# A two-layer encoder in 3-product fp32: five instead of four seven-product couples in each wide pair, other weight sums, and evictions by ScalarE

## The chip, the cores and the metric

One core of a Trainium2 chip runs the whole program. The metric is the device time of one execution in microseconds. The engines are TensorE (PE; its weight loads are PEld), VectorE (DVE), ScalarE (ACT), GpSimd (POOL) and SyncE (SP), whose queue issues the loads.

## The reference

Two layers over 256 positions of width 2048, all in float32. A layer is a mixing half (projection, windowed attention, pooling, output projection) and a feed-forward half. Only the feed-forward half changes here:

```
x = x + rms_norm(mixed, g_mix_post)
f = square(relu(rms_norm(x, g_ffn_pre) @ w_up)) @ w_down      # 2048 -> 8192 -> 2048
x = x + rms_norm(f, g_ffn_post)
```

## The kernel before

**Three matmuls for a product.** Each float32 operand is split into a high part, rounded to the fast format fp32r, and a low remainder. For weights ScalarE casts (`w_hi<-raw`), VectorE subtracts (`w_lo<-raw,w_hi`). A product of a 128x128 stationary block and a 128x512 moving block is three matmuls, high x high, high x low, low x high (`three`, L870). In what follows a "product" is these three.

**Groups.** D_FF = 8192 is done in four groups g = 0 to 3 of 2048 columns. In each, four up units compute `relu(h @ w_up)^2` (`turned_unit`; the last one, u = 3, is `last_unit` on the other engines), and then two *wide pairs* q = 0 and 1 multiply it by w_down: each pair makes 1024 output columns (two banks of 512 for each of two token tiles, `acc_pair[t][:, c]`) over the 16 k-tiles of the group. In group 3 the place of pair 1 is taken by two narrow units. So there are 7 wide pairs in a layer, 14 in all.

**Slots and couples.** A wide pair takes its 16 k-tiles as slots i = 0 to 15, one 128x1024 piece of w_down each. Plain slots take four products (t, c). Two neighbouring slots can be a *couple* (`seven`, L880): a 2x2x2 block product with seven products in place of eight, as in Strassen's scheme. It needs sums of the four weight blocks (`weight_sums` on VectorE: `t_sum`, and one that overwrites half of `raw`, the "third"), split in turn into `t_hi` (ScalarE, 128x1536) and `t_lo` (VectorE, 128x1536), and four sums of activation blocks (`s_sum`, `s_hi`, `s_lo`), made in the up units. Four of the seven products go to banks shared by all couples (`ssa_bank`, two `t_bank`, `o_bank`); the two that use `t_hi` for them are `shared_products`. They are added to `kept_sums` once a group (`shared_sums`). In the kernel before the couples stand at slots 0, 4, 8 and 12 of each pair.

**Rings.** `raw` has 4 slots, `w_hi` and `w_lo` 8. SP reloads a raw slot when the `w_lo` made from it is done (`lo_made`); ScalarE casts into a `w_hi` slot when TensorE has used it (`w_used`). There are two buffers each of `t_hi` and `t_lo`.

**Order of the work.** Each engine's order is written out by hand. On VectorE `last_unit` and then `wide_pair` for q = 0 and 1 stand one behind the other; the sums `wide_sums` (L1937) empty the four banks of a pair and come after the first slots of the next. `bank_free` lets TensorE write a bank again only then. The buffer `t_hi` of couple 1 overlaps `act_f`, so its cast waits until the last up unit's `f_lo` is made (`flo_made`).

Of the kernel before, what the change touches and what calls it, by code (L numbers as in the profile page):

```python
# [139 lines left out]
SEVEN_AT = (0, PAIRS, RING, RING + PAIRS)  # L140
SEVEN_UNIT = ((1, 0), (1, 1), (2, 0), (2, 1))
K_ORDER = (4, 5, 0, 1, 6, 7, 2, 3, 8, 9, 12, 13, 10, 11, 14, 15)
SHARED = 4


def pair_at(g, q):

    return (q + g + 1) % 2


def seven_no(l, g, q, n):

    return ((l * WIDE_LAYER) + g * 2 + q) * len(SEVEN_AT) + n
# [12 lines left out]
def wide_done(l, g, q):  # L166

    return l * WIDE_LAYER + g * 2 + q + 1
# [8 lines left out]
def build(nc, x_in, positions, g_mix_pre, w_in, g_attn_out, w_pool, pool_scale, g_pool_out,  # L177
# [13 lines left out]
    def own(name, shape, dtype=F32):  # L191
# [65 lines left out]
    t_lo = [at(f"t_lo{n}", [P, 3, CH], F32R, low) for n, (_, low) in enumerate(r_t)]  # L257
    r_s = ((r_qkv + 36 * CH, r_qkv + 40 * CH), (r_qkv + 44 * CH, r_xg), (r_xg + 4 * CH, r_post),
           (r_post + 4 * CH, r_post + 8 * CH))
# [26 lines left out]
    rt = [own(f"rt{n}", [P, T, ROPE // 2]) for n in range(6)]  # L286
    rt_i = own("rt_i", [P, T, ROPE // 2], I32)
    pos_f = own("pos_f", [P, T])
    freq = own("freq", [P, ROPE // 2])
# [5 lines left out]
    t_bank = [nc.alloc_psum_tensor(f"t_bank{n}", [P, CH], F32) for n in range(2)]  # L295
    o_bank = nc.alloc_psum_tensor("o_bank", [P, CH], F32)
    ssa_bank = nc.alloc_psum_tensor("ssa_bank", [P, CH], F32)
# [95 lines left out]
    with nc.Block() as block:  # L393
# [3 lines left out]
        def _(sp):  # L397
# [33 lines left out]
            def load_wide(l, g, j, hu):  # L431

                for i in range(SLOTS):
# [3 lines left out]
                    src = w_down[ld(l, 1), ld(g * D + K_ORDER[i] * P, P), ld(j * 2 * CH, 2 * CH)]  # L437
# [3 lines left out]
            def load_group(l, g, last=False):  # L441
# [3 lines left out]
                load_wide(l, g, pair_at(g, 0), hu + 2 * CHUNKS)  # L445
                if not last:
                    load_wide(l, g, pair_at(g, 1), hu + 2 * CHUNKS + PAIR_HALVES)
                    return
# [72 lines left out]
        def _(pe):  # L521
# [163 lines left out]
            for l in range(DEPTH):  # L685
# [194 lines left out]
                def seven(g, q, n, hu, result):  # L880

                    i = SEVEN_AT[n]
                    no, s0, s1 = seven_no(l, g, q, n), i % RING, i % RING + 1
                    k0, k1 = K_ORDER[i], K_ORDER[i + 1]
                    first = n == 0
                    begin, end = first and (q == 1 or g == 0), n == len(SEVEN_AT) - 1 and q == 0
# [3 lines left out]
                    th, tl = t_hi[n % 2], t_lo[n % 2]  # L890
                    if q == 0:
                        pe.wait_ge(flo_made, l * 32 + g * 8 + k1 // 2 + 1)
                        pe.wait_ge(s_lo_made, (l * FF_GROUPS + g) * len(SEVEN_AT) + n + 1)
# [1517 lines left out]
```

## Time and profile before

| | |
|---|---|
| median of 3 runs | 1889.77 us (1889.09 to 1890.19) |
| profiled execution | 1889.38 us, its span 1887.3 us |
| busy, share of span | PE 1874.9 us (99%), DVE 1497.9 (79%), ACT 1111.4 (59%), POOL 118.5 (6%) |
| granted clock of TensorE, mean | 0.999 |
| chain that ended last | PE 95%, DVE 3%, issue 1% |
| one product's three matmuls | 379 ns each; starts 0.216 us apart |

Matmuls are pipelined: the duration of one is 379 ns, but the next starts 0.216 us after it, so counts are multiplied by the distance of starts. VectorE's and ScalarE's instructions overlap a little too: the distance of two starts is some 0.09 us less than the duration.

### The profile page before, as it was taken

To read this page: it belongs to the slowest core of one execution; us is meant where nothing else is said; L and a number is where in the kernel's file an instruction comes from. 1 tells how busy PE (TensorE), PEld (TensorE's weight loads), DVE (VectorE), ACT (ScalarE), POOL (GpSimd) and SP (SyncE) were. 2 spreads that over 40 slices of the span, in tenths; PEclk is the share of its full clock that TensorE was granted. 3 is DMA by queue.
4 is the path that set the end of the run, shared out by engine and by line. 5 is a ranking of instruction groups with operands and counts; after the bars stand their busy time and mean duration, and the time that the engine had idled before them with its cause. 6 is when DMAs were issued, how large, how long until landed. Compare 5 with 4: busy or idle time off the path is not lost.

```text
span 1887.3 us, 27369 instructions
## 1 busy us (share of the span) xinstructions
PE 1874.9 (99%) x9950; PEld 1672.1 (89%) x9950; DVE 1497.9 (79%) x1885; ACT 1111.4 (59%) x1485; POOL 118.5 (6%) x166
## 2 busy tenths in 40 slices
PE   9999999999999999999999999999999999999998
PEld 7988988988988998898888888889889889989987
DVE  6886657898699689788877757678977996897886
ACT  6455656855665565566554556568556655645662
POOL 3920010000000000000000000100000000000000
PEclk9999999999999999999999999999999999999999
DMA  8665366757566666767576554586676666567673
GB/s 290 201 221 181 112 201 226 236 182 255 189 198 216 214 198 195 236 202 241 210 234 225 187 168 134 170 275 194 197 236 207 195 212 221 183 207 235 221 257 124
DMA packets 170068, 390.92 MB, mean 207 GB/s; under 512 B 12161, under 2 KB 14321, under 8 KB 168433
## 3 DMA queue, kind: packets, MB, share of 16 engines
q1 hardware_dynamic: 167904, 377.58, 61.8%
q10 hardware_dynamic: 2064, 12.08, 1.7%
q8 instruction: 56, 0.92, 0.2%
q14 instruction: 44, 0.35, 0.1%
HBM read 382.53 MB, written 7.08 MB: 206 GB/s over the span
## 4 chain that ended last, share of the span: by engine, by line
PE 95%; DVE 3%; issue 1%; ACT 0%; DMA 0%; POOL 0%; DVEq 0%; POOLq 0%; ACTq 0%
PE acc_pair L573 25%; PE acc_pair L578 13%; PE acc_pair L539 8%; PE acc_pair L540 8%; PE acc_pair L541 8%; PE acc_pair L874 7%; PE acc_pair L873 7%; PE acc_pair L872 7%; DVE w_lo L1445 1%; PE t_bank L874 1%; PE t_bank L873 1%; PE t_bank L872 1%; PE o_bank L791 1%; DVE h_both L1501 1%; PE ssa_bank L872 1%
## 5 line engine op out<-in xcount | busy, mean ns | idle before, releaser
L995 ACT CAST w_hi<-raw 128x1024 fp32r<-128x1024 f32 x687 | 703.6, 1048 | 476.4 <-DVE raw L1998 190.7
L1445 DVE TENSOR_TENSOR w_lo<-raw,w_hi 128x1024 fp32r<-128x1024 f32 x687 | 827.4, 1232 | 169.0 <-ACT w_hi L995 161.8
L573 PE MATMUL acc_pair<-h_both,w_hi 128*128 128x512 f32 x2176 | 560.3, 380 | 0.2
L573 PEld LDWEIGHTS acc_pair<-h_both,w_hi 128*128 128x128 f32 x2176 | 371.4, 190 | 30.4 <-issue 0.5
L578 PEld LDWEIGHTS acc_pair<-h_both,w_lo 128*128 128x128 f32 x2176 | 327.4, 190 | 29.2
L578 PE MATMUL acc_pair<-h_both,w_lo 128*128 128x256 f32 x2176 | 330.5, 274 | 0.0
L872 PE MATMUL acc_pair<-w_hi,f_hi 128*128 128x512 f32 x504 | 191.0, 379 | 0.0
L873 PE MATMUL acc_pair<-w_lo,f_hi 128*128 128x512 f32 x504 | 191.0, 379 | 0.0
L874 PE MATMUL acc_pair<-w_hi,f_lo 128*128 128x512 f32 x504 | 191.0, 379 | 0.0
L539 PE MATMUL acc_pair<-w_hi,h_both 128*128 128x512 f32 x444 | 170.4, 384 | 1.8 <-DVE w_lo L1445 1.6
L540 PE MATMUL acc_pair<-w_lo,h_both 128*128 128x512 f32 x444 | 168.3, 379 | 0.0
L541 PE MATMUL acc_pair<-w_hi,h_both 128*128 128x512 f32 x444 | 168.3, 379 | 0.0
L539 PE MATMUL acc_pair<-w_hi,f_hi 128*128 128x512 f32 x384 | 148.0, 385 | 0.0
L540 PE MATMUL acc_pair<-w_lo,f_hi 128*128 128x512 f32 x384 | 145.5, 379 | 0.0
L541 PE MATMUL acc_pair<-w_hi,f_lo 128*128 128x512 f32 x384 | 145.5, 379 | 0.0
L2013 DVE TENSOR_TENSOR t_lo<-t_sum,t_hi 128x1536 fp32r<-128x1536 f32 x56 | 98.1, 1753 | 12.4 <-ACT t_hi L1325 12.4
L872 PEld LDWEIGHTS acc_pair<-w_hi,f_hi 128*128 128x128 f32 x504 | 95.3, 189 | 13.5
L874 PEld LDWEIGHTS acc_pair<-w_hi,f_lo 128*128 128x128 f32 x504 | 95.3, 189 | 13.5
L873 PEld LDWEIGHTS acc_pair<-w_lo,f_hi 128*128 128x128 f32 x504 | 95.3, 189 | 13.5
L2223 POOL TENSOR_TENSOR rstd<-mean_sq,minus_half 128x1 f32<-128x1 f32 (+1 forms) x16 | 13.5, 843 | 1407.8 <-DVE ss_post L1460 1135.5
L539 PEld LDWEIGHTS acc_pair<-w_hi,h_both 128*128 128x128 f32 x444 | 83.9, 189 | 15.7 <-issue 2.9
L541 PEld LDWEIGHTS acc_pair<-w_hi,h_both 128*128 128x128 f32 x444 | 83.9, 189 | 12.0
(252 smaller groups left out, 2293.8 us busy)
## 6 DMA issues: line engine op xcount, KB each, us to landing
raw<-in_w_up SPq DMA_DIRECT2D x256, 512.0 KB, 4.4
raw<-in_w_down SPq DMA_DIRECT2D x240, 512.0 KB, 5.0
raw<-in_w_in SPq DMA_DIRECT2D x128, 512.0 KB, 4.7
raw<-in_w_out SPq DMA_DIRECT2D x64, 512.0 KB, 5.3
raw_side<-in_w_down SPq DMA_DIRECT2D x16, 512.0 KB, 7.0
x_kept<-x ACTq DMA_DIRECT2D x4, 1024.0 KB, 6.2
x<-x_kept ACTq DMA_DIRECT2D x4, 1024.0 KB, 6.1
x<-in_x SPq DMA_DIRECT2D x8, 256.0 KB, 7.5
```

The source lines that it names most:

```text
L539: pe.matmul(bank[:, :], xh, wh, start=begin and k == 0, stop=False)
L540: pe.matmul(bank[:, :], xh, wl, start=False, stop=False)
L541: mm = pe.matmul(bank[:, :], xl, wh, start=False, stop=end and k == 1)
L573: pe.matmul(acc_pair[b][:, m, :], w_hi[:, slot, col:col + P], x_both.rearrange("p s (a n) -> p s n a", a=2), start=(slot, k) == (0, 0), st ...
L578: mm = pe.matmul(acc_pair[b][:, m, 0:SEQ], w_lo[:, slot, col:col + P], x_hi.rearrange("p (a n) -> p n a", a=2), start=False, stop=(slot, k ...
L791: mm = pe.matmul(o_bank[:, e * SEQ:(e + 1) * SEQ], proj[:, 6 + h // 4, kt, h_cols(h % 4)], probs_t[:, e, kt, :], start=kt == 0, stop=kt == 1)
L872: pe.matmul(bank, xh, in_turn(wh), start=start, stop=False)
L873: pe.matmul(bank, xh, in_turn(wl), start=False, stop=False)
L874: return pe.matmul(bank, xl, in_turn(wh), start=False, stop=stop)
L995: act.copy(w_hi[:, half * PAIRS + p, :], raw[:, p, :]).then_inc(hi_made, 1)
L1445: dve.tensor_tensor(w_lo[:, slot, :], src[:, p, :], w_hi[:, slot, :].bitcast(F32), ALU.subtract).then_inc(lo_made, 1)
L2013: dve.tensor_tensor(t_lo[n % 2][:, :, :], t_sum[n % 2][:, :, :], t_hi[n % 2][:, :, :].bitcast(F32), ALU.subtract).then_inc(t_lo_made, 1)
```

## The change

- Couples in a wide pair: five in place of four, at slots 0, 4, 6, 10, 12 of pair 0 and 0, 4, 8, 12, 14 of pair 1. A fifth set of activation sums (unit u = 3) is made in `last_unit`.
- Weight sums: the third first (`weight_third`), then one sum, then two in one 128x1024 instruction with a broadcast operand. Three instructions of VectorE in place of four.
- The thirds of couples 1 and 2 and the sums of couple 1 stand in `last_unit`; the sums of couple 2 (slots 6 and 7) stand behind it.
- Shared banks: copied by ScalarE in groups 0 and 1, added by VectorE in one 128x2048 instruction in groups 2 and 3. The first sums of a layer (group 0) are written by ScalarE.

```diff
-SEVEN_AT = (0, PAIRS, RING, RING + PAIRS)
+SEVEN_AT = ((0, 4, 6, 10, 12), (0, 4, 8, 12, 14))
+SEVEN_UNIT = ((1, 0), (1, 1), (2, 0), (2, 1), (3, 0))[:max(COUPLES)]
...
+                    if (q, i) == (0, 10) and 6 in SEVEN_AT[0]:
+                        sp.wait_ge(t_step, 2 * seven_no(l, g, 0, 2) + 2)
...
                 def last_unit(g):            # ScalarE
-                    seven_hi(g, 0, 0, hu + 2, 0)
+                    two_hi(g, 0, 0)
+                    sums_hi(g, 0, 0)
+                    two_hi(g, 0, 2)
                     s_rest(g, 3)
                     take_half(g, u, 0)
                     turned_hi(g, u, 0)
-                    act.wait_ge(t_third, seven_no(l, g, 0, 1) + 1)
-                    split_hi(hu + 3, 1, (0, 1))
+                    two_hi(g, 0, 4)
                     take_half(g, u, 1)
-                    split_hi(hu + 3, 1, (2, 3))
+                    two_hi(g, 0, 6)
                     turned_hi(g, u, 1)
+                    s_rest(g, 4)
                     sums_hi(g, 0, 1)
+                    sums_hi(g, 0, 2)
...
+                def first_shared(g):         # ScalarE, groups 0 and 1
+                    act.wait_ge(t_used, 3 * seven_no(l, g, 0, COUPLES[0]) - 1)
+                    for k in range(SHARED):
+                        act.copy(kept_sums[:, 1 - pair_at(g, 0), k, :], shared[:, k, :]
+                                 ).then_inc(shared_free, 1)
...
+                def weight_third(g, q, n):   # VectorE
+                    dve.tensor_tensor(top_r, low_r, top_r, ALU.subtract).then_inc(t_third, 1)
+                def weight_sums(g, q, n):
+                    dve.wait_ge(t_third, no + 1)
+                    dve.tensor_tensor(out[:, 0, :], top[:, c_cols(1)], top[:, c_cols(0)], ALU.add
+                                      ).then_inc(t_step, 1)
+                    dve.wait_ge(t_step, 2 * no + 1)
+                    dve.tensor_tensor(out[:, 1:3, :], low, out[:, 0:1, :].to_broadcast([P, 2, CH]),
+                                      ALU.subtract).then_inc(t_step, 1)
+                def couple_lo(g, q, i):
+                    weight_sums(g, q, n)
+                    two_lo(g, q, i)
+                    if i + 2 in SEVEN_AT[q]:
+                        weight_third(g, q, n + 1)
+                    sums_lo(g, q, n)
...
                 def wide_pair(g, q, first, last=False):
+                    if q == 0 and 6 in SEVEN_AT[0]:
+                        weight_sums(g, 0, 2)
+                        two_lo(g, 0, 8)
+                        sums_lo(g, 0, 2)
+                    wide_lo(g, q, (10 if 6 in SEVEN_AT[0] else 8, 4)[q])
                     if q == 0 and not last:
+                        weight_third(g, 1, 0)
+                        couple_lo(g, 1, 0)
+                        if g >= T:
+                            shared_sums(g)
+                        two_lo(g, 1, 2)
+                        if not first:
+                            wide_sums(g, q)
```

VectorE from the second half of the last up unit into pair 0, in the kernel before (L1914 takes the unit's result, L1924 is `f_lo`, L1445 is `w_lo`, L1995 to L2007 are the weight sums of a couple):

```order
L1924 TENSOR_TENSOR f_lo<-act_f,f_hi 128x512 [waits fhi_made,f_ready]
L1445 TENSOR_TENSOR w_lo<-raw,w_hi 128x1024 [waits hi_made] x2
L1914 TENSOR_TENSOR act_f<-acc_pair,act_f 128x512 [waits half_taken]
L1445 TENSOR_TENSOR w_lo<-raw,w_hi 128x1024 [waits hi_made] x2
L1924 TENSOR_TENSOR f_lo<-act_f,f_hi 128x512 [waits fhi_made,f_ready]
L2013 TENSOR_TENSOR t_lo_96<-t_sum_94,t_hi_92 128x1536 [waits t_hi_made]
L1995 TENSOR_TENSOR t_sum_93<-raw 128x512 [waits raw_loaded0,t_used]
L1998 TENSOR_TENSOR raw<-raw 128x512 [waits raw_loaded1]
L2002 TENSOR_TENSOR t_sum_93<-raw,t_sum_93 128x512 [waits t_used,t_step]
L2007 TENSOR_TENSOR t_sum_93<-raw,t_sum_93 128x512 [waits t_used,t_step]
L1445 TENSOR_TENSOR w_lo<-raw,w_hi 128x1024 [waits hi_made] x2
L2013 TENSOR_TENSOR t_lo_95<-t_sum_93,t_hi_91 128x1536 [waits t_hi_made]
```

The same place in the changed kernel (L1991 takes the result, L2001 is `f_lo`, L1522 is `w_lo`, L2068 is the third, L2083 and L2088 are the sums, L2057 is the fifth `s_lo`):

```order
L1522 TENSOR_TENSOR w_lo<-raw,w_hi 128x1024 [waits hi_made] x2
L1991 TENSOR_TENSOR act_f<-acc_pair,act_f 128x512 [waits half_taken]
L2068 TENSOR_TENSOR raw<-raw 128x512 [waits raw_loaded3,raw_loaded2]
L1522 TENSOR_TENSOR w_lo<-raw,w_hi 128x1024 [waits hi_made] x2
L2001 TENSOR_TENSOR f_lo<-act_f,f_hi 128x512 [waits fhi_made,f_ready]
L2057 TENSOR_TENSOR s_lo_111<-s_sum_106,s_hi_101 128x512 [waits s_hi_made]
L2095 TENSOR_TENSOR t_lo_96<-t_sum_94,t_hi_92 128x1536 [waits t_hi_made]
L2083 TENSOR_TENSOR t_sum_93<-raw 128x512 [waits t_third,t_used]
L2088 TENSOR_TENSOR t_sum_93<-raw,t_sum_93 128x1024 [waits t_used,t_step]
L1522 TENSOR_TENSOR w_lo<-raw,w_hi 128x1024 [waits hi_made] x2
L2095 TENSOR_TENSOR t_lo_95<-t_sum_93,t_hi_91 128x1536 [waits t_hi_made]
```

The third of couple 2 now stands before the `w_lo` of slots 6 and 7, and its `t_lo` (the last row) stands behind the `w_lo` of slots 8 and 9. Couple 2 stands at slot 6 in place of slot 8.

ScalarE at the same place in the kernel before (L1292 takes the result, L1299 to L1303 are relu, square and `f_hi`, L1325 is `t_hi`):

```order
L1292 COPY act_f<-acc_pair 128x512 [waits flo_made,w_used]
L995 CAST w_hi<-raw 128x1024 [waits w_used,raw_loaded2]
L995 CAST w_hi<-raw 128x1024 [waits w_used,raw_loaded3]
L1299 ACTIVATE act_f<-act_f 128x512 [waits acc_free1]
L1301 ACTIVATE act_f<-act_f 128x512 [waits relu_made]
L1303 CAST f_hi<-act_f 128x512 [waits f_ready]
L1325 CAST t_hi_92<-t_sum_94 128x1536 [waits t_step,flo_made]
L995 CAST w_hi<-raw 128x1024 [waits w_used,raw_loaded0,t_third]
L995 CAST w_hi<-raw 128x1024 [waits w_used,raw_loaded1]
L1325 CAST t_hi_91<-t_sum_93 128x1536 [waits t_step]
```

And in the changed kernel (L1022 is `w_hi`, L1337 the fifth `s_hi`, L1389 `t_hi`):

```order
L1319 COPY act_f<-acc_pair 128x512 [waits flo_made,w_used]
L1022 CAST w_hi<-raw 128x1024 [waits w_used,raw_loaded2,t_third]
L1022 CAST w_hi<-raw 128x1024 [waits w_used,raw_loaded3]
L1326 ACTIVATE act_f<-act_f 128x512 [waits acc_free1]
L1328 ACTIVATE act_f<-act_f 128x512 [waits relu_made]
L1330 CAST f_hi<-act_f 128x512 [waits f_ready]
L1337 CAST s_hi_101<-s_sum_106 128x512 [waits s_step]
L1389 CAST t_hi_92<-t_sum_94 128x1536 [waits t_step,flo_made]
L1389 CAST t_hi_91<-t_sum_93 128x1536 [waits t_step]
L1022 CAST w_hi<-raw 128x1024 [waits w_used,raw_loaded0]
L1022 CAST w_hi<-raw 128x1024 [waits w_used,raw_loaded1]
```

The cast of slot 6 now waits for a third as well, and the `t_hi` of couple 2 stands between the `t_hi` of couple 1 and the casts of slots 8 and 9.

## Rows read from the trace of the kernel before

**Rows 1.** Waits: whose idle time TensorE had in total, times, longest.
```profile
PE acc_pair L539 <- DVE w_lo L1445: 1.6, 4, 0.4
```

**Rows 2.** Windows, group 2 of layer 0: up units, then wide pairs; busy us per engine.
```profile
619.00:701.00 82.00, 82.00 (x501) 75.26 (x501) 59.63 (x76) 50.35 (x64) 0.00 (x0) 1.00 0.64 205
701.00:780.00 79.00, 78.91 (x368) 68.86 (x367) 71.96 (x77) 44.66 (x45) 0.00 (x0) 1.00 0.66 209
```

**Rows 3.** Timeline of TensorE (start, us, what): pair 0, pair 1, next unit begin.
```profile
701.34 0.38 PE L872 MATMUL ssa_bank<-w_hi,s_hi 128*128 128x512 f32 x1
...
740.19 0.38 PE L872 MATMUL ssa_bank<-w_hi,s_hi 128*128 128x512 f32 x1
...
779.29 1.12 PE L573 MATMUL acc_pair<-h_both,w_hi 128*128 128x512 f32 x4
```

**Rows 4.** Timeline of VectorE, same group: start, us, what, idle before and releaser.
```profile
685.48 0.28 DVE L1965 TENSOR_TENSOR s_sum<-act_f 128x128 f32<-128x128 f32 x1
...
686.54 0.69 DVE L1924 TENSOR_TENSOR f_lo<-act_f,f_hi 128x512 fp32r<-128x512 f32 x1
...
702.93 0.68 DVE L1914 TENSOR_TENSOR act_f<-acc_pair,act_f 128x512 f32<-128x512 f32 x1
703.53 2.35 DVE L1445 TENSOR_TENSOR w_lo<-raw,w_hi 128x1024 fp32r<-128x1024 f32 x2
...
708.19 1.76 DVE L2013 TENSOR_TENSOR t_lo<-t_sum,t_hi 128x1536 fp32r<-128x1536 f32 x1 [1.54 <-ACT t_hi L1325]
709.87 0.69 DVE L1995 TENSOR_TENSOR t_sum<-raw 128x512 f32<-128x512 f32 x1
710.47 0.69 DVE L1998 TENSOR_TENSOR raw<-raw 128x512 f32<-128x512 f32 x1
711.07 0.68 DVE L2002 TENSOR_TENSOR t_sum<-raw,t_sum 128x512 f32<-128x512 f32 x1
711.79 0.69 DVE L2007 TENSOR_TENSOR t_sum<-raw,t_sum 128x512 f32<-128x512 f32 x1
712.40 2.35 DVE L1445 TENSOR_TENSOR w_lo<-raw,w_hi 128x1024 fp32r<-128x1024 f32 x2
714.67 1.75 DVE L2013 TENSOR_TENSOR t_lo<-t_sum,t_hi 128x1536 fp32r<-128x1536 f32 x1
716.34 2.35 DVE L1445 TENSOR_TENSOR w_lo<-raw,w_hi 128x1024 fp32r<-128x1024 f32 x2
...
719.94 0.69 DVE L1998 TENSOR_TENSOR raw<-raw 128x512 f32<-128x512 f32 x1 [0.65 <-DMA raw<-in_w_down]
...
777.74 2.72 DVE L1937 SCALAR_TENSOR_TENSOR acc<-acc_pair,rstd,acc 128x512 f32<-128x512 f32 x4
```

**Rows 5.** Timeline of ScalarE, same group, around the start of pair 0.
```profile
701.54 0.59 ACT L1292 COPY act_f<-acc_pair 128x512 f32<-128x512 f32 x1
702.02 2.00 ACT L995 CAST w_hi<-raw 128x1024 fp32r<-128x1024 f32 x2
703.92 0.62 ACT L1299 ACTIVATE act_f<-act_f 128x512 f32<-128x512 f32 x1
...
705.24 0.62 ACT L1303 CAST f_hi<-act_f 128x512 fp32r<-128x512 f32 x1
706.69 1.47 ACT L1325 CAST t_hi<-t_sum 128x1536 fp32r<-128x1536 f32 x1 [0.83 <-DVE f_lo L1924]
```

**Rows 6.** Groups by form on VectorE: busy, mean ns, idle before, releaser.
```profile
L2013 DVE TENSOR_TENSOR t_lo<-t_sum,t_hi 128x1536 fp32r<-128x1536 f32 x56 | 98.1, 1753 | 12.4 <-ACT t_hi L1325 12.4
...
L1998 DVE TENSOR_TENSOR raw<-raw 128x512 f32<-128x512 f32 x56 | 38.5, 688 | 10.2 <-DMA raw<-in_w_down 10.1
...
L1703 DVE TENSOR_TENSOR pooled<-pooled_all,u_t 128x512 f32<-128x512 f32 x8 | 9.1, 1140 | 0.3
...
L1452 DVE TENSOR_TENSOR xg<-o_bank,gain 128x512 f32<-128x512 f32 x8 | 5.5, 692 | 28.9 <-ACT o_sq L1233 28.9
```

**Rows 7.** Window of the last 17 us: busy times, then granted clock.
```profile
1870.00:1887.30 17.30, 9.05 (x42) 7.58 (x41) 7.51 (x15) 0.96 (x4) 1.08 (x2) 0.85 0.35 121
```

## What the change will do to the time: the prediction

> **What bounds the kernel now.** I read the page's shares first: TensorE is busy 99% of the span. Then its waits: for weights it waits 1.6 us in the whole run [rows 1], so no other engine sets the time of the feed-forward half. But the cover is uneven. In the up units VectorE is busy 59.6 us of 82, in the wide pairs 72.0 of 79 [rows 2]. So VectorE, whose work the change increases just there, is the engine to follow; it can be behind TensorE only by what stands in the ring, and its waits show how much of a stage it can still take up.
>
> Times are those of group 2 of layer 0. Pair 0 starts on TensorE at 701.34, pair 1 at 740.19, the next up unit at 779.29 [rows 3]. A pair is 4 x 7 + 4 x 8 = 60 products, so a product costs 38.85 / 60 = 0.6475 us.
>
> **What the change removes.** One product in each of 14 pairs: 14 x 0.6475 = 9.1 us of TensorE. If everything stayed covered, that would be the gain, and it is the most that the change can give.
>
> **What it adds to VectorE.** Prices are distances of starts [rows 4]: a 512-wide operation 0.60 us (709.87 to 710.47), 0.72 where it needs the one before (711.07 to 711.79), a 1024-wide one 2.27 / 2 = 1.135, a 1536-wide one 1.67 (714.67 to 716.34). The four old sums of a couple cost 2.53 us; the three new ones 0.72 + 0.72 + 1.135 = 2.58, if the broadcast is free. It was free in the 512-wide product with `gain` (692 ns), while the `pooled` operation took 1140 ns for 512 [rows 6]; these are the two ends for it, and I take the first, since its operand is broadcast too. So the new sums save nothing, and a fifth couple adds 2.58 + 1.67 = 4.25 us to VectorE in each pair, plus 1.06 for the activation sums (685.48 to 686.54) and 0.60 for their low part in the last up unit. The shared sums as one 128x2048 operation I put at 2.2 us (0.53 for each 512 more, from 1024 at 1.22 and 1536 at 1.75), against 2.4 for four.
>
> The Trainium skill (VectorE: DVE Perf Modes, "The TRN2 errata") says that a float32 `tensor_tensor` of N elements takes (N+151)/0.96 ns, a fixed 157 ns that two operations in one pay once. The durations of the rows agree (691 ns for 512), but their starts are only 0.60 apart, so most of the fixed part is hidden already. By the page a couple would save 0.09 us more, some 0.7 us in a group, and the sum would be about 4 us lower.
>
> **The first wait, step by step.** In the last up unit VectorE has no wait to absorb the activation sums. So it takes the unit's second result at 702.93 + 1.06 = 703.99. Then comes the third of couple 2, 704.6 to 705.3. The cast of slot 6 waits for it: ScalarE casts slots 6 and 7 from 705.3, and goes on after 1.9 us (702.02 to 703.92) with relu, square and `f_hi`, which take 705.86 - 703.92 = 1.94 us [rows 5]. `f_hi` ends at 709.15, `f_lo` at 709.9. Now `t_hi` of couple 1 may start (in the kernel before it started at 706.69): it ends at 711.4. VectorE: `t_lo` of couple 1 at 711.4, sums of couple 2 at 713.1 and 713.8, ending at 715.05. ScalarE: `t_hi` of couple 2 to 716.5, then the cast of slot 8, done at 717.5, since it now stands behind. VectorE, idle for 2.5 us, makes `w_lo` of slots 8 and 9 from 717.5, and only at 719.8 `t_lo` of couple 2, ready at 721.55.
>
> TensorE wants it at slot 6, after 7 + 8 + 7 + 4 = 26 products: 701.34 + 16.84 = 718.2. It waits 3.4 us. This chain has no part that depends on the group: `t_lo` waits for `t_hi` 12.4 us in all, which is 8 times the 1.54 of the row shown [rows 4, 6]. So 8 x 3.4 = 27 us.
>
> **The rest of the wide stage.** From 719.8 until the first two banks of pair 1 are emptied, VectorE has in group 2: 8 `t_lo` (13.4), 7 couples' sums (17.8: two thirds stand alone at 0.60), 24 `w_lo` (27.2), the shared sums (2.2), four bank sums (2.6, at 0.66: 777.74, 2.72 for four) and two more (1.4). Together 64.6 us. It also waits for loads. A piece lands 5.2 us after the `w_lo` that frees its place (714.75 to 719.94, where it idled 0.65), and the third, which needs it, now stands first and not second: 0.65 + 0.60 = 1.25 us at the first couple of pair 1 and at its slots 8 and 12, 3.7 us. 719.8 + 64.6 + 3.7 = 788.1. The next up unit needs those banks, and started at 779.29 before, 0.14 us after the same two sums. So group 2 is 8.8 us longer. TensorE's waits for it: 3.4 at slot 6, 3.7 for the shared banks at the start of pair 1, and some 3 spread over the banks, the last couples and the next unit.
>
> Group 1: ScalarE copies the shared banks. That takes 2.2 off VectorE, but the casts of slots 2 and 3 stand behind the copies and cost it 0.7. 7.3 us longer. Group 0: VectorE is rid of the bank sums too; its waits are 3.4, 1.1 for the copies (they stand behind a `t_hi` that ends at 742), 1.4 at slot 14 and 1.1 at slot 2 of the next unit, whose cast stands behind ScalarE's four sums: 7.0 - 1.3 = 5.7. Group 3 has one pair and no couples behind it: 3.4 + 1.2 (bank sums behind the wider shared sum) - 0.65 = 3.9.
>
> A layer: 8.8 + 7.3 + 5.7 + 3.9 = 25.7, two layers 51.4. The up units have 22 us without work on VectorE [rows 2], so nothing is carried from group to group. The profiled execution took 1889.4, the median is 1889.8, which are the same here; 1889.4 + 51.4 = 1941.
>
> **The rivals.**
> - *Cover holds.* TensorE never waits: 1889.4 - 9.1 = 1880. For it: it never waited before. Against it: only 7 us without work on VectorE in the wide stage [rows 2], and 2 x 4.25 us more work in it, besides 1.7 us more ahead of it. It needs the first chain to be 3.4 us shorter. 7%.
> - *Only the first wait.* VectorE makes up the rest while TensorE stands: 1889.4 - 9.1 + 27 = 1907. It needs VectorE's 68 us to shrink by 5, say loads that land sooner. 14%.
> - *Broadcast at half speed.* The two-in-one sum takes 2 x 1.14 = 2.28 in place of 1.22, 1.06 more for each of 8 couples in six groups and one in two: 53 us on top, 1994. 5%.
> - *The clock falls.* After each of the eight longer waits TensorE runs at 1.2 GHz for as much work as it missed, and 3.4 us of work take 6.8: 27 us more, 1968. Against it, the granted clock is 1.00 in both stages [rows 2], and 0.85 only in the last 17 us, where TensorE was busy for 9 [rows 7]. Part would fall into waits that are there anyway. 8%. The Trainium skill (TensorE: Matmul & The Clock Gate, "What's actually happening") says that the throttled state is the default and activity releases it, which speaks for this rival; no row here has full work behind a long wait.
> - *Balance.* Waits that give back just the 9.1: no change. 3%.
>
> **How the numbers follow.** My case has 63%, its own range 1920 to 1960: one step off by 0.1 us on each of 70 couples is 7 us, and a load that lands 0.5 us later at three places in six groups is 9. The range for 8 in 10 reaches down to the first wait alone, 1905, and up past the clock's case, 1975. A measurement here tells 0.2% (3.8 us) from nothing. Faster by more: the first rival, 7%. Within: 3%. Slower: the rest, 90%.
>
> **What would show it.** In the new profile TensorE's waits name `t_lo` 8 times with about 3.4 us each; if they are absent, the first chain is wrong. Waits for the shared sums come at the start of pair 1, longest in group 2, none in group 3. VectorE's busy share in the wide stage rises above 90%. The 1024-wide sum has 1.22 us, or my price for the broadcast is wrong. Matmuls of the 512 form are 42 fewer. The forecast fails if VectorE shows idle time in the wide pairs while TensorE has none.

## The result: 3.3% slower, and the profile after

The changed kernel takes 1952.1 us (median of 4 runs, 1951.9 to 1952.6) against 1889.8 for the kernel before: ratio 1.033, 95% interval 1.0313 to 1.0346. The forecast was 1941 us, range 1905 to 1975, so direction and range hold and the size was 11 us short. The profiled execution spans 1950.0 us, 62.7 more than before.

The page: busy time by engine, then the chain that ended last.

```profile
PE 1891.5 (97%) x9908; PEld 1674.2 (86%) x9908; DVE 1546.5 (79%) x1881; ACT 1157.0 (59%) x1539; POOL 117.7 (6%) x166
...
PE 64%; DVE 21%; DMA 7%; issue 5%; ACT 3%; DVEq 0%; POOL 0%; POOLq 0%; ACTq 0%; SPq 0%
```

There are 42 matmuls fewer, as forecast, and yet TensorE is busy 17 us longer, in the main because 71 of them ran slowly (below). The chain was TensorE's for 95%; now 64% of it is, 21% is VectorE's and 7% the loads'.

TensorE's longest waits (who waits for whom; us in total, times, longest), which answer to [rows 1]:

```profile
PE shared L894 <- DVE t_lo L2095: 28.0, 8, 3.6
PE shared L894 <- DVE w_lo L1522: 9.3, 6, 1.8
PE shared L894 <- DVE kept_sums L2128: 3.9, 2, 2.0
```

Before, it waited 1.6 us for VectorE in all. Now it waits 28.0 for `t_lo` alone, eight times and at most 3.6: one wait in each pair 0, at slot 6. TensorE's timeline of group 2, layer 0 [rows 3] has pair 0, the wait, pair 1 and the next up unit:

```profile
717.57 0.38 PE L894 MATMUL shared<-w_hi,s_hi 128*128 128x512 f32 x1
...
738.01 0.74 PE L894 MATMUL shared<-t_hi,s_hi 128*128 128x512 f32 x1 [3.44 <-DVE t_lo L2095]
...
763.20 0.48 PE L894 MATMUL shared<-w_hi,s_hi 128*128 128x512 f32 x1 [1.87 <-DVE kept_sums L2128]
...
804.58 1.13 PE L595 MATMUL acc_pair<-h_both,w_hi 128*128 128x512 f32 x4 [0.56 <-DVE acc L2009]
```

So the wait ends 20.4 us after the start of pair 0, pair 1 starts at 45.6 and the next unit at 87.0. The forecast had 20.2 (721.55 - 701.34) and 86.8 (788.1 - 701.34).

VectorE's timeline there, to be laid beside [rows 4]; the number in brackets is its idle time and who ended it:

```profile
730.22 1.22 DVE L2088 TENSOR_TENSOR t_sum<-raw,t_sum 128x1024 f32<-128x1024 f32 x1
733.93 2.36 DVE L1522 TENSOR_TENSOR w_lo<-raw,w_hi 128x1024 fp32r<-128x1024 f32 x2 [2.48 <-ACT w_hi L1022]
736.21 1.75 DVE L2095 TENSOR_TENSOR t_lo<-t_sum,t_hi 128x1536 fp32r<-128x1536 f32 x1
737.87 0.68 DVE L2068 TENSOR_TENSOR raw<-raw 128x512 f32<-128x512 f32 x1
738.66 0.69 DVE L2083 TENSOR_TENSOR t_sum<-raw 128x512 f32<-128x512 f32 x1
739.39 1.23 DVE L2088 TENSOR_TENSOR t_sum<-raw,t_sum 128x1024 f32<-128x1024 f32 x1
740.53 2.36 DVE L1522 TENSOR_TENSOR w_lo<-raw,w_hi 128x1024 fp32r<-128x1024 f32 x2
...
754.26 0.69 DVE L2068 TENSOR_TENSOR raw<-raw 128x512 f32<-128x512 f32 x1 [1.03 <-DMA raw<-in_w_down]
...
777.84 0.69 DVE L2068 TENSOR_TENSOR raw<-raw 128x512 f32<-128x512 f32 x1 [0.93 <-DMA raw<-in_w_down]
...
787.74 0.69 DVE L2068 TENSOR_TENSOR raw<-raw 128x512 f32<-128x512 f32 x1 [0.94 <-DMA raw<-in_w_down]
```

The row at 733.93 is the forecast's first chain: VectorE stands 2.48 us until the casts of slots 8 and 9 are done. ScalarE's two rows say why, `t_hi` of couple 2 first and the casts behind it [rows 5]:

```profile
731.48 1.48 ACT L1389 CAST t_hi<-t_sum 128x1536 fp32r<-128x1536 f32 x1 [3.69 <-DVE t_sum L2088]
732.86 1.98 ACT L1022 CAST w_hi<-raw 128x1024 fp32r<-128x1024 f32 x2
```

Only at 736.21 does VectorE make the `t_lo` that TensorE wants. Behind that stand three waits for loads, 2.9 us in all. The groups of VectorE (busy us, mean ns, idle before and releaser), for [rows 6]:

```profile
L2095 DVE TENSOR_TENSOR t_lo<-t_sum,t_hi 128x1536 fp32r<-128x1536 f32 x70 | 122.6, 1752 | 7.9 <-ACT t_hi L1389 7.9
...
L2088 DVE TENSOR_TENSOR t_sum<-raw,t_sum 128x1024 f32<-128x1024 f32 x70 | 85.8, 1225 | 2.4
...
L2068 DVE TENSOR_TENSOR raw<-raw 128x512 f32<-128x512 f32 x70 | 48.0, 686 | 21.1 <-DMA raw<-in_w_down 20.9
...
L2128 DVE TENSOR_TENSOR kept_sums<-shared,kept_sums 128x2048 f32<-128x2048 f32 x4 | 9.1, 2283 | 0.0
```

The broadcast is free (1225 ns for 1024), and the thirds wait 20.9 us for loads in place of 10.1.

How much longer (in us) each group is than before, from the start of its wide stage to the start of the next group's; group 3 is taken to the end of its one wide pair. From the starts on TensorE's timeline:

| group | forecast | layer 0 | layer 1 |
|---|---|---|---|
| 0 | 5.7 | 7.0 | 7.2 |
| 1 | 7.3 | 8.1 | 8.6 |
| 2 | 8.8 | 9.1 | 9.3 |
| 3 | 3.9 | 6.0 | 6.5 |

Together these are 61.7 us of the 62.7. Another 1.1 stands ahead of the first product of the program (13.84 against 12.70) and need not be the change's: in the experiments' traces that start lay between 12.6 and 13.7. (The stretches behind group 3 give 0.2 back.)

### The profile page after: what moved, and what is told of

The parts are those of the page before. It is cut to its first block, busy times and chain, and to the rows that moved or that the text cites. A ratio compares the mean times of both kernels' runs of the same rounds, so it can differ in the third digit from the quotient of the medians.

```text
span 1950.0 us, 27385 instructions
## 1 busy us (share of the span) xinstructions
PE 1891.5 (97%) x9908; PEld 1674.2 (86%) x9908; DVE 1546.5 (79%) x1881; ACT 1157.0 (59%) x1539; POOL 117.7 (6%) x166
## 4 chain that ended last, share of the span: by engine, by line
PE 64%; DVE 21%; DMA 7%; issue 5%; ACT 3%; DVEq 0%; POOL 0%; POOLq 0%; ACTq 0%; SPq 0%
PE acc_pair L595 22%; PE acc_pair L600 11%; DVE w_lo L1522 8%; PE acc_pair L561 8%; PE acc_pair L563 8%; PE acc_pair L562 8%; DMA raw<-in_w_down 7%; DVE t_sum L2088 4%; DVE t_sum L2083 2%; DVE raw L2068 2%; DVE t_lo L2095 1%; ACT w_hi L1022 1%; DVE acc L2009 1%; PE shared L813 1%; DVE h_both L1578 1%
## 5 line engine op out<-in xcount | busy, mean ns | idle before, releaser
L1522 DVE TENSOR_TENSOR w_lo<-raw,w_hi 128x1024 fp32r<-128x1024 f32 x687 | 827.8, 1232 | 191.1 <-ACT w_hi L1022 183.9
L1022 ACT CAST w_hi<-raw 128x1024 fp32r<-128x1024 f32 x687 | 702.6, 1049 | 458.0 <-DVE raw L2068 201.8
L894 PE MATMUL acc_pair<-w_hi,f_hi 128*128 128x512 f32 x406 | 155.9, 384 | 0.1
L895 PE MATMUL acc_pair<-w_lo,f_hi 128*128 128x512 f32 x406 | 155.3, 382 | 0.0
L896 PE MATMUL acc_pair<-w_hi,f_lo 128*128 128x512 f32 x406 | 154.6, 381 | 0.0
L561 PE MATMUL acc_pair<-w_hi,f_hi 128*128 128x512 f32 x384 | 148.2, 386 | 1.2 <-DVE acc L2009 1.2
L562 PE MATMUL acc_pair<-w_lo,f_hi 128*128 128x512 f32 x384 | 145.5, 379 | 0.0
L563 PE MATMUL acc_pair<-w_hi,f_lo 128*128 128x512 f32 x384 | 145.5, 379 | 0.0
L1389 ACT CAST t_hi<-t_sum 128x1536 fp32r<-128x1536 f32 x70 | 103.4, 1478 | 56.0 <-DVE t_sum L2088 51.0
L2095 DVE TENSOR_TENSOR t_lo<-t_sum,t_hi 128x1536 fp32r<-128x1536 f32 x70 | 122.6, 1752 | 7.9 <-ACT t_hi L1389 7.9
L561 PEld LDWEIGHTS acc_pair<-w_hi,h_both 128*128 128x128 f32 x444 | 83.9, 189 | 15.4 <-issue 2.5
L563 PEld LDWEIGHTS acc_pair<-w_hi,h_both 128*128 128x128 f32 x444 | 83.9, 189 | 11.9
L562 PEld LDWEIGHTS acc_pair<-w_lo,h_both 128*128 128x128 f32 x444 | 84.0, 189 | 11.0
L894 PEld LDWEIGHTS acc_pair<-w_hi,f_hi 128*128 128x128 f32 x406 | 77.8, 192 | 12.4 <-DVE acc L2009 0.9
```

Source lines behind the costliest of these rows:

```text
L561: pe.matmul(bank[:, :], xh, wh, start=begin and k == 0, stop=False)
L562: pe.matmul(bank[:, :], xh, wl, start=False, stop=False)
L563: mm = pe.matmul(bank[:, :], xl, wh, start=False, stop=end and k == 1)
L894: pe.matmul(bank, xh, in_turn(wh), start=start, stop=False)
L895: pe.matmul(bank, xh, in_turn(wl), start=False, stop=False)
L896: return pe.matmul(bank, xl, in_turn(wh), start=False, stop=stop)
```

## The experiments

Theory A is the forecast's: the order of ScalarE and VectorE around slot 6, and then VectorE's work and its loads. Against it stood that the first wait is all (B), that a fifth couple costs the same wherever it stands (C), and later that the low clock behind the waits costs the time (K). Where an expectation splits A, A1 is VectorE's work and A2 the loads. Each diff is against the changed kernel, and its median (1952.1) is what the numbers are compared with unless the text says otherwise.

**1. The couple of slot 6 at slot 8.**
```diff
-SEVEN_AT = ((0, 4, 6, 10, 12), (0, 4, 8, 12, 14))
+SEVEN_AT = ((0, 4, 8, 10, 12), (0, 4, 8, 12, 14))
```


> Pair 0 has its five couples at slots 0, 4, 8, 10, 12 in place of 0, 4, 6, 10, 12; pair 1 as in the changed kernel. So the chain that made couple 2 late at slot 6 is gone, and its cast stands where it stood before. Theory A (a chain at slot 6, and beside it a wide stage that VectorE can no longer keep up with): the waits of 3.5 us go, and with them the slow matmuls behind them (8 x 3.5 + 8 x 1.7 = 42 us off 1952), the waits at the start and end of pair 1 stay: 1911, range 1905 to 1918. Theory B (all later waits only follow from the first): TensorE never waits, 1881. Theory C (a fifth couple costs the same wherever it stands): 1940 to 1952.

Measured: 1922.2 us, 1.0177 (1.016 to 1.0194) of before, and no wait for a `t_lo`. Waits that are left:

```profile
PE shared L894 <- DVE w_lo L1522: 9.1, 9, 1.7
PE shared L894 <- DVE kept_sums L2128: 6.9, 2, 3.5
PE acc_pair L561 <- DVE acc L2009: 5.1, 2, 2.6
```

The place of one couple is worth 29.9 us. The edit moves more than the slot: with no couple at slot 6, its third and sums also leave the stretch around the last up unit. VectorE does the same work, but no longer stands 2.5 us before the `w_lo` of slot 8. The other 32 us stay. B (1881) and C (1940 to 1952) fell; A had 21 us here (1911, range 1905 to 1918) and was too low too, outside its range.

**2. Four couples with the new sums, evictions and order.**
```diff
+SEVEN_AT = ((0, 4, 8, 12), (0, 4, 8, 14))
```


> Four couples in each pair again (0, 4, 8, 12 and 0, 4, 8, 14), but with the new weight sums, the wide shared sum and ScalarE's evictions. Theory A: TensorE waits for about 1 us in group 0 and hardly elsewhere, so as before the change: 1892, range 1889 to 1896. Rival (the new sums or ScalarE's evictions cost time by themselves): over 1898.

1893.4 us, 1.0016 (1.0007 to 1.0026), as A has it. The other parts of the change cost 3 us together; all the rest comes with the fifth couple. The thirds wait 39.5 us for loads here, more than the 20.9 of the changed kernel, and hardly anything is lost: such a wait costs time only where VectorE sets the pace.

**3. ScalarE casts slots 8 and 9 ahead of the `t_hi` of couple 2.**
```diff
                     if 6 in SEVEN_AT[0]:
+                        two_hi(g, 0, 8)
                         sums_hi(g, 0, 2)
...
-                    wide_hi(g, 0, 8)
+                    wide_hi(g, 0, 10)
```


> The changed kernel with one thing moved on ScalarE: the casts of slots 8 and 9 stand before the t_hi of couple 2, not behind it. VectorE then makes w_lo of slots 8 and 9 while t_hi is cast, and t_lo is ready 2.5 us sooner. The wait at slot 6 falls from 3.5 to about 0.8 us and the clock stays full behind it: 8 x 1.7 = 14 us. Theory A1 (after slot 6 the rate of VectorE's work sets the stage): each group ends 2.6 us sooner as well, 1952 - 14 - 21 = 1917. Theory A2 (the loads into the four raw slots set the rate, so the time comes back as waits at slots 10 to 15): only the clock's part, 1938, range 1933 to 1944.

1949.2 us, 1.0313 (1.0296 to 1.033): hardly a gain, and outside both expectations (1917, and 1933 to 1944). Yet the first wait nearly went (TensorE's waits), and VectorE's 2.48 us with it. Where they went, a row of VectorE's timeline in group 2, its wait for loads in the whole run and a wait of the load queue show:

```profile
PE shared L894 <- DVE w_lo L1523: 18.8, 14, 1.6
PE shared L894 <- DVE kept_sums L2129: 7.4, 2, 3.8
PE shared L894 <- DVE t_lo L2096: 7.3, 8, 1.0
```

```profile
735.81 0.69 DVE L2069 TENSOR_TENSOR raw<-raw 128x512 f32<-128x512 f32 x1 [1.99 <-DMA raw<-in_w_down]
```

```profile
DVE raw L2069 <- DMA raw<-in_w_down: 36.5, 28, 2.0
SPq L458 <- DVE t_sum L2089: 85.8, 8, 11.0
```

VectorE came to the third of the next couple earlier and waited for its load: 36.5 us for loads in place of 20.9. The last row says why this cure could not help there. The change lets the load of slot 10 go out only behind the sums of couple 2, whose raw slots it overwrites. In group 2 they end at 729.9, the load is issued at 729.96, and the third of slots 10 and 11 starts at 735.81; casting slots 8 and 9 earlier moves none of these. That suggests theory L (A2 above): casts, sums, `w_lo` and the reload of one of four `raw` slots are a loop, and time won inside it is given back at the load.

**4. Only half of each wide piece is loaded.** It leaves out the right 512 columns of `w_down`'s pieces.
```diff
+   src = w_down[ld(l, 1), ld(g * D + K_ORDER[q][i] * P, P), ld(j * 2 * CH, CH)]
+   sp.dma_start(raw[:, p, 0:CH], ...)
```


> The changed kernel, but each load of a wide pair brings only the left 512 columns of its piece (256 of 512 KB); the right half stays what it was, so the products are not those of the reference. All engines do the same work. Theory A2 (the loop of load, third, cast, w_lo and the next load sets the rate of the wide stage): VectorE's waits for loads (20.9 us in the changed kernel) nearly vanish, and six groups end 2 to 3 us sooner, 1935 to 1940. Theory A1 (VectorE's work alone sets it): 1948 to 1953.

1934.6 us, 1.0235 (1.0218 to 1.0252), just below A2's 1935 to 1940: the size of the loads carries 17.5 us. Window of group 2 from the `t_lo` that ends the first wait to the next unit, in the changed kernel, then here (window, its length, busy us of PE, PEld, DVE, ACT, POOL, granted clock, DMA share, GB/s):

```profile
736.21:804.58 68.37, 62.46 (x277) 52.77 (x277) 64.71 (x62) 35.80 (x33) 0.00 (x0) 0.98 0.61 188
```

```profile
732.41:797.61 65.20, 62.90 (x276) 53.96 (x277) 64.44 (x62) 35.73 (x33) 0.00 (x0) 0.95 0.37 117
```

With half loads VectorE is busy 64.4 of 65.2 us: in this window its work alone sets the pace. The 3.2 us more in the changed kernel are its three waits for loads (2.9) and little else.

**5. Experiments 3 and 4 together.** (Only the left columns are loaded.)

> ScalarE's casts of slots 8 and 9 stand ahead of the t_hi of couple 2 (alone 1949.2), and only the left 512 columns of each wide piece are loaded (alone 1934.6), so results are not the reference's. Theory L (the loads took back what the earlier casts gave): with half loads VectorE's 2.5 us of idle time before the w_lo of slot 8 goes and no load wait of 2.0 takes its place; the wide stage of group 2 falls from 83.84 to about 81.5, eight pairs save 2.3 to 2.5 each, and the time is 1915 (1911 to 1921). Rival V (VectorE's idle time there costs nothing, the rest of its work sets the pace anyway): 1930 to 1935.

1916.5 us, 1.0142 (1.0125 to 1.0159). With half loads the earlier casts bring 18.1 us (1934.6 to 1916.5); with full loads they brought 2.9. VectorE's waits:

```profile
DVE raw L2069 <- DMA raw<-in_w_down: 2.4, 6, 0.6
```

This is L's number (1915), and it shows that the loads took the gain of experiment 3. It is not made up as L said, though. The two groups 0 give 5.3 and 3.9 us of it and the other six 1.3 to 2.4 each, where eight times 2.3 to 2.5 was expected; experiment 7 shows what is special in group 0.

**6. Work in place of the long wait.** Five more products are made before the wait of slot 6 and added to an output bank, so that bank holds more than it should.
```diff
+                        if (q, n) == (0, 2):
+                            for _ in range(5):
+                                three(acc_pair[0][:, 0, :], ..., False, False)
                         shared_products()
```


> The changed kernel, in which TensorE does five more products (15 matmuls, 3.2 us) into a bank of its own just before it waits for t_lo at slot 6; one product is thereby added six times. TensorE is busy in the place of its wait, so its clock has no reason to fall; nothing else waits differently, since VectorE's t_lo is as late as before. The time taken off is what the slow clock cost. Theory K1 (the slow matmuls behind each of the eight waits, 8 to 14 of them at 0.21 us more, are paid in full): 8 x 2.2 = 18 us, 1934. Theory K2 (later waits for VectorE take most of it back, and only groups 3 and 0 pay): 2 x (2.0 + 1.0 + 0.5) = 7 us, 1945. Theory K0 (the clock costs nothing): 1952.

1960.8 us, 1.0374 (1.0355 to 1.0394): slower by 8.7, outside all three (K1 1934, K2 1945, K0 1952). Two of TensorE's waits, and a row of its timeline at the start of pair 1, group 2:

```profile
PE shared L894 <- DVE kept_sums L2133: 7.5, 2, 4.1
...
PE shared L894 <- DVE t_lo L2100: 2.1, 8, 0.3
```

```profile
765.77 0.80 PE L894 MATMUL shared<-w_hi,s_hi 128*128 128x512 f32 x1 [4.11 <-DVE kept_sums L2133]
```

The waits for `t_lo` are 2.1 us and no slow matmul stands behind them. But TensorE, now early, waits for the shared sums 4.11 and not 1.87. So what the low clock took was taken from a wait that comes anyway. The edit disturbed something else too: the thirds waited 27.9 us for loads, against 20.9 in the changed kernel. Whether these 7.0 are most of the 8.7, and why the loads came later, is open.

By itself this run can't tell a clock that costs nothing from a cost that the later loads hide. Waits within one kernel do, since the clock did not fall behind all of them. In experiment 9 (below), which has full loads too, none of the matmuls behind the waits of 3.60 us (group 1 of layer 0) and 3.64 (group 0 of layer 1) is slow, and these wide stages take 86.5 and 84.2 us. Their twins in the other layer, with 6 and 13 slow matmuls, take 86.8 and 83.7. In experiment 4 the wide stages of the two groups 1 take 82.23 us each, with no slow matmul behind the wait of 3.44 in layer 0 and 9 in layer 1. Where VectorE sets the end, the slow matmuls have no price.

**7. The same with half loads.** (Both leave-outs of 4 and 6.)

> Both edits at once: five more products (added to an output bank) stand ahead of the wait of couple 2 at slot 6, and only the left 512 columns of each wide piece are loaded, so results are not the reference's. Theory L (the way of the loads through four raw slots sets the pace of the changed kernel, and hides there what the lower clock costs): with half loads that cover is gone and the lower clock is on the path; in that kernel 12 or 13 matmuls start 0.427 us apart and not 0.216 behind a wait of 3.44, so 2.7 us at each of eight waits, 21 us. Filled with work, the waits shrink to 0.2 to 0.3 us, no slow matmul stands behind them, and the time falls from 1934.6 to about 1913 (1908 to 1920). Rival V (VectorE's work sets the pace with half loads too): the time stays above 1930, and TensorE waits later by what it was early.

1938.0 us, 1.0257 (1.0241 to 1.0273). My theory said 1913 here and fell; the rival said above 1930. But one part of the theory holds. ScalarE has taken over VectorE's sums in group 0, and there the wide stage does get shorter with the waits filled, from 83.3 to 80.5 us and from 81.7 to 80.2, a little more than the 12 and 6 slow matmuls behind its two waits of experiment 4 took (2.5 and 1.3 us). Five of the other six wide stages get longer, by 0.4 to 1.5 us; why is open. So with half loads VectorE's work covers the slow matmuls in groups 1 and 2, and in group 0 they are paid. With full loads (experiment 6) group 0 does not get shorter (83.7 and 83.9 us, 83.5 and 83.7 in the changed kernel).

**8. ScalarE's evictions given back to VectorE.** VectorE copies the four shared banks in groups 0 and 1 in one instruction and makes the first bank sums.
```diff
-                        if g >= T:
-                            shared_sums(g)
+                        shared_sums(g)
...
-                        if not first:
-                            wide_sums(g, q)
+                        wide_sums(g, q)
```


> The changed kernel with ScalarE's part undone: VectorE copies the shared banks in groups 0 and 1 (one 128x2048 copy) and writes the first sums of each pair in group 0. Theory A (VectorE is late in the wide stage): groups 0 and 1 become as long as group 2 (87.0 us for 84.7 and 85.8), 2 x (2.5 + 1.2) = 7 us more, 1960, range 1957 to 1964. Rival (ScalarE's evictions save nothing, since its own casts are late for them): 1950 to 1954.

1960.3 us, 1.0377 (1.0359 to 1.0394), as A has it. In each layer the edit lengthens group 0 by some 3 us and group 1 by 1: VectorE's work is on the path, and this part of the change is worth 8 us.

**9. The two-in-one sum as two instructions.**
```diff
-dve.tensor_tensor(out[:, 1:3, :], low, out[:, 0:1, :].to_broadcast([P, 2, CH]), ALU.subtract)
+dve.tensor_tensor(out[:, 1, :], low[:, 0, :], out[:, 0, :], ALU.subtract)
+dve.tensor_tensor(out[:, 2, :], low[:, 1, :], out[:, 0, :], ALU.subtract)
```


> The two-in-one sum of a couple is done as two operations of 128x512. Their starts would be 2 x 0.60 = 1.20 us against 1.14 (739.39 to 740.53), so 0.06 us more for each of 70 couples on VectorE. Theory L (casts, sums, w_lo and loads form one loop): the sums lie in it, and the time rises by 0 to 4 us, to 1952 to 1957. Rival D (each instruction has a fixed cost that the duration shows: 2 x 0.689 against 1.225, 0.15 more): 70 x 0.15 = 11 us more, 1963. Rival N (VectorE's work is off the path): no change.

1955.3 us, 1.0345 (1.033 to 1.0361), 3.2 more than the changed kernel, whose interval (1.0313 to 1.0346) overlaps this one. Its two sums and the `w_lo` behind them:

```profile
740.14 0.69 DVE L2088 TENSOR_TENSOR t_sum<-raw,t_sum 128x512 f32<-128x512 f32 x1
740.75 0.68 DVE L2089 TENSOR_TENSOR t_sum<-raw,t_sum 128x512 f32<-128x512 f32 x1
741.35 2.35 DVE L1522 TENSOR_TENSOR w_lo<-raw,w_hi 128x1024 fp32r<-128x1024 f32 x2
```

Two take 1.21 us of starts, one takes 1.14 (739.39 to 740.53): 70 x 0.07 = 4.9 us of VectorE. The 3.2 us measured do not tell 4.9 from nothing with certainty, but the durations (2 x 0.69 against 1.225) would say 11, and that is excluded.

**10. GpSimd makes the thirds.**
```diff
 def weight_third(g, q, n):      # VectorE: empty
...
+                            pool.tensor_tensor(top_r, low_r, top_r, ALU.subtract
+                                               ).then_inc(t_third, 1)
```


> The changed kernel, with the third of each couple made by GpSimd as soon as the two pieces have landed (about 1.3 us each) and not by VectorE. It takes 0.6 us a couple off VectorE and its waits for loads. Theory A1 (VectorE's work sets the stage): some 6 us of work and 3 us of waits less in each of six groups, 1952 - 50 = about 1900. Theory A2 (the loop load, third, cast, w_lo, next load on four raw slots sets it): the third only takes 0.7 us longer in the loop, 1940 to 1955.

1970.9 us, 1.0434 (1.0417 to 1.0451), outside both expectations (1900, and 1940 to 1955). By form (busy us, mean ns, idle):

```profile
L1522 DVE TENSOR_TENSOR w_lo<-raw,w_hi 128x1024 fp32r<-128x1024 f32 x687 | 846.7, 1260 | 184.0 <-ACT w_hi L1022 176.6
...
L2487 POOL TENSOR_TENSOR raw<-raw 128x512 f32<-128x512 f32 x70 | 107.2, 1531 | 1004.2 <-DMA raw<-in_w_down 1004.2
```

```profile
DVE t_sum L2078 <- POOL raw L2487: 68.4, 36, 2.9
```

A third takes 1531 ns on average in place of 686, the casts and sums behind it come later, and VectorE waits 68.4 us for it. The work left VectorE and stayed in the loop. The averages mix two cases. The shortest third takes 1.26 us and most take less than 1.35, but some up to 2.30, and of VectorE's 687 `w_lo` 17 take 2.30 us where the rest take 1.22, each beside a third. Here is one; the first of its two `w_lo` is the long one, 3.44 us for what takes 2.35 elsewhere:

```profile
722.28 1.37 POOL L2487 TENSOR_TENSOR raw<-raw 128x512 f32<-128x512 f32 x1 [3.48 <-DMA raw<-in_w_down]
722.43 3.44 DVE L1522 TENSOR_TENSOR w_lo<-raw,w_hi 128x1024 fp32r<-128x1024 f32 x2
```

**11. Four couples in pair 0, five in pair 1.**
```diff
+SEVEN_AT = ((0, 4, 8, 12), (0, 4, 8, 12, 14))
```


> Four couples in pair 0 (0, 4, 8, 12), five in pair 1 (0, 4, 8, 12, 14): six products fewer than in the kernel before, 3.9 us of TensorE. Theory A (a fifth couple in pair 1 costs VectorE 4.3 us, of which the idle time of the kernel before takes most): small waits at slot 14, at the next unit's banks and in group 0 at its slot 2, 2.5 us a layer after the saving, 1895, range 1892 to 1899. Rival (each fifth couple costs the same, half of 62 us): 1920.

1898.4 us, 1.0048 (1.0031 to 1.0065), as A has it. Even a fifth couple without the wait of slot 6 does not pay: TensorE makes 8 products more than the changed kernel but 6 fewer than the kernel before (3.9 us), and waits 10.5 us for VectorE in place of 1.6.

**12. The best form found.**
```diff
+SEVEN_AT = ((0, 4, 10, 12), (0, 4, 8, 12, 14))
...
-                        split_hi(hu + 16, 0, (0, 1))
+                        split_hi(hu + 16, 0)
                         if first:
                             first_sums(1)
-                        split_hi(hu + 16, 0, (2, 3))
```


> Couples at slots 0, 4, 10, 12 of pair 0 (four) and 0, 4, 8, 12, 14 of pair 1 (five), and ScalarE's last two copies of a bank sum in group 0 stand behind all four casts of the next unit. From the kernel with couples at 0, 4, 8, 12 and five in pair 1 (1898.4): it had 5.4 us of waits in layers' up units and 1.1 in the second slot of the unit behind group 0, which the moved copies should take away (2 x 1.1), and pair 0 with its third couple at slot 10 gives VectorE 4 us more time before pair 1. Expected 1891 (1888 to 1897). Rival: the fifth couple in pair 1 alone makes VectorE late, and it stays at 1898.

1892.6 us, 1.0012 (1.0003 to 1.0021), within the expected bounds. Six products are saved (3.9 us), and TensorE waits 4.6 us for VectorE in place of 1.6; by these two it should be 0.9 us faster than the kernel before, and it is 2.8 slower (1889.8 beside it); what takes the rest is open. No version here beats the kernel before.

## Why the prediction was right, and where its size was off

**What is removed.** 14 products, 42 matmuls, 9.1 us: right by count. The experiments do not measure it by itself.

**The first chain.** Right to 0.2 us: eight waits of 3.44 to 3.6 for `t_lo`, forecast 3.4, with its parts where they were put (2.48 idle, forecast 2.5). Experiment 1 shows that the place of couple 2 is worth 29.9 us, and 3 that ScalarE's order makes most of the wait (28.0 us fall to 7.3). What the forecast didn't say: curing the wait alone gives 2.9 us.

**VectorE's price of a couple.** Forecast 2.58, measured 2.66 (737.87 to 740.53), and the broadcast free. The Trainium skill (VectorE: DVE Perf Modes, "The TRN2 errata") gives each float32 `tensor_tensor` a fixed 151 cycles, 157 ns, so that two in one would save as much (an estimate from that figure). The durations here agree (1225 ns for 1024, 2283 for 2048), the time doesn't: experiment 9 splits 70 of them and costs 3.2 us and not 70 x 0.157 = 11.

**Group 2.** 68.3 us were forecast from 719.8 to the next unit (64.6 of work and 3.7 of loads); measured 68.37 from 736.21, made up of 65.5 and 2.9. That the sum is right to 0.1 us is luck: the work was put 0.9 too low (the 0.08 that each couple costs more is over half of it) and the loads 0.8 too high. The waits fell otherwise than put: 1.9 us for the shared sums instead of 3.7, since TensorE, slowed behind the first wait, came to them later.

**Group 3, the largest miss.** Of the 11 us that the forecast was short, groups 0 to 3 have 2.8, 2.1, 0.8 and 4.7. In group 3 forecast 3.9 us, measured 6.0 and 6.5. The step that failed reads "3.4 + 1.2 (bank sums behind the wider shared sum) - 0.65". ScalarE's rows at the end of that pair:

```profile
923.62 1.05 ACT L1022 CAST w_hi<-raw 128x1024 fp32r<-128x1024 f32 x1 [2.16 <-DMA raw<-in_w_down]
927.02 1.05 ACT L1022 CAST w_hi<-raw 128x1024 fp32r<-128x1024 f32 x1 [2.35 <-DMA raw<-in_w_down]
```

The pieces of the narrow unit behind the pair come singly, each cast waits for its load, and VectorE's bank sums stand behind their `w_lo`, where VectorE waits up to 2.17 us for a cast. In this place I had counted VectorE's work and no load. In experiment 4, where these pieces are loaded whole, group 3 of layer 0 still takes 44.85 us (44.86 in the changed kernel), which agrees. No run takes these waits away, so this cause is read from the rows and not shown by an experiment.

**Groups 0 and 1.** 1.3 and 1.5, and 0.8 and 1.3 us too low. The wait in group 0's next unit is as put: its up stage is 85.0 us and not 83.8, and I had counted 1.1 there. So the miss lies in its wide stage. There the forecast wait of 1.1 us for ScalarE's copies is absent from the trace, and slow matmuls stand in its place, about 1.5 us behind each `t_lo`. Where the clock stays high, in group 0 of layer 1 of experiment 9, the wait for the copies comes, with 1.1 us. What makes groups 0 and 1 longer than put I did not isolate.

**The clock rival.** Its mechanism is real, and in the changed kernel its price is nil. TensorE's windows around the wait of group 0 (clock is the third number from the end), then its timeline there:

```profile
398.00:401.00 3.00, 0.83 (x2) 0.74 (x3) 2.90 (x4) 0.25 (x1) 0.00 (x0) 0.86 0.85 247
401.00:404.00 3.00, 3.00 (x9) 2.40 (x9) 2.97 (x4) 2.94 (x3) 0.00 (x0) 0.57 0.40 132
404.00:420.00 16.00, 16.00 (x76) 14.01 (x75) 14.68 (x14) 8.35 (x9) 0.00 (x0) 1.00 0.64 196
```

```profile
401.61 0.63 PE L894 MATMUL shared<-t_hi,s_hi 128*128 128x512 f32 x1
402.04 0.63 PE L895 MATMUL shared<-t_lo,s_hi 128*128 128x512 f32 x1
...
403.68 0.38 PE L896 MATMUL acc_pair<-t_hi,f_lo 128*128 128x512 f32 x1
403.89 0.38 PE L894 MATMUL acc_pair<-w_hi,f_hi 128*128 128x512 f32 x1
```

In the changed kernel, behind each wait of 3.44 us or more 6 to 13 matmuls start 0.427 us apart and not 0.216, which is 1.2 GHz in place of 2.4. In the run these are 71 matmuls, 71 x 0.211 = 15 us of TensorE. The rival had 27. The Trainium skill (TensorE: Matmul & The Clock Gate, "What's actually happening") has the low state as the default that activity lifts. The rows agree so far: the granted clock fell behind the wait and is 1.00 again in the third window, with TensorE at work throughout. But experiments 6 and 7 took the slow matmuls behind these waits away and the time did not fall, and stages of one kernel with and without slow matmuls are equally long. VectorE sets the end, and TensorE makes up a slow stretch in its next wait. Only in group 0 with half loads was it paid.

**The other rivals.** Cover, first wait only, broadcast at half speed and balance all fell. The first wait alone (1907) needed loads that land sooner, and they do not suffice: with half loads the first wait stands as it was (27.8 us for `t_lo`) and the time is 1934.6.

**Signs badly chosen.** VectorE's share of the wide stage was to rise above 90%. It is 78.3 of 87.0 us, 90.0%, and by [rows 2] it had been 72.0 of 79.0, 91%, before the change. The stage grows with the work, so the share says nothing; idle time inside the stage does. Of the waits for shared sums at the start of pair 1 only those of group 2 are there (1.9 and 2.0 us).

## What to carry to other kernels

When TensorE's cover is used up, follow the engine behind it through the whole stage: its work, its waits for the other engines, and the loop through which its buffers come back. A wait that is cured inside such a loop may be given back at the next link, so halve the suspected link (here the loads) and repeat the cure before counting on it. Time lost on an engine that has a later wait is no time lost, whatever its clock, as far as that wait reaches: stage by stage, not for the whole kernel at once.

## What the runs showed of the hardware that I had not expected

- How long TensorE waits does not decide whether it then runs slowly. In all these traces there are 57 waits of 2.4 to 4.6 us. Behind 47 of them stand 5 to 13 slow matmuls, behind ten (2.47 to 3.64 us) none. Of shorter waits only one, of 1.89 us in experiment 10, has slow ones behind it (8). In experiment 4 two waits of 3.44 us differ, in group 1 and then in group 2 of layer 0 (clock is the third number from the end):

```profile
569.00:572.00 3.00, 3.00 (x15) 2.63 (x14) 2.97 (x4) 2.94 (x3) 0.00 (x0) 1.00 0.01 2
735.00:738.00 3.00, 3.00 (x9) 2.37 (x8) 2.97 (x4) 2.94 (x3) 0.00 (x0) 0.50 0.04 16
```

- When GpSimd makes the thirds (128x512 in float32), VectorE's `w_lo` take 1260 ns on average in place of 1232 and its `t_lo` 1814 in place of 1752. No instruction is a little slower: 17 `w_lo` take 2.30 us in place of 1.22 and four `t_lo` 2.83 in place of 1.75, all beside a third, and the others are as fast as ever. An average over a line can hide a few instructions that are 1.08 us late.
- Halving each wide piece brings a load's landing from 4.9 us to 3.1 (medians from issue to landing), not to half.
